# Attention products with the values stationary, two heads in the two 64-column halves of the array

## The reference, cut to what matters

```python
s = einsum('bghnqe,bghnke->bghnqk', qs, kb) * (Dh ** -0.5) + bias      # masked with -inf
p = exp(s - max(s)); l = sum(p)
o = einsum('bghnqk,bghnke->bghnqe', p / l, vb);  lse = m + log(l)
wts = softmax(stack(lses, axis=0), axis=0)        # over the 3 groups
y_a = sum(wts[..., None] * stack(outs, axis=0), axis=0)      # [256, 6 * 64]
merged = sigmoid(gate_a) * (y_a @ w_attn_proj) + sigmoid(gate_b) * (y_b @ w_ret_proj)
```

## Time and profile before

| | |
|---|---|
| median of 3 runs | 2450.14 us |
| lowest, highest | 2447.23, 2452.81 us |
| span of the profiled execution | 2447.4 us |
| busy in it | PE 2127.8, PEld 1525.4, DVE 785.8, ACT 703.8, POOL 1002.4 us |
| mean granted TensorE clock | 0.910 |
| attention of layer 0 (first scores to last ya) | 1372 to 1492 us |
| attention of layer 1 | 1947 to 2067 us |

### The profile page before, as it was taken

The page is one execution under the profiler, slowest core; times in us unless marked ns, Lnnn a source line. Parts: engine busy times, 40 slices in busy tenths (PEclk is TensorE's granted clock), DMA queues, the critical chain, the costliest instruction groups (busy, mean ns, idle before and its releaser), DMA issues.

```text
span 2447.4 us, 31903 instructions
## 1 busy us (share of the span) xinstructions
PE 2127.8 (87%) x13416; PEld 1525.4 (62%) x13416; DVE 785.8 (32%) x1516; ACT 703.8 (29%) x820; POOL 1002.4 (41%) x324
## 2 busy tenths in 40 slices
PE   7999988766777766776659999999999999999998
PEld 4788973333333333332318888887887887888887
DVE  4575752111111111111121435533312253634231
ACT  2246410000000000000004544544543453644442
POOL 1356530000000000000007765887887764786885
PEclk9999988788777888778879999999999999999999
DMA  9585479999999999999996544566656643555653
GB/s 329 152 282 164 156 325 399 428 428 428 428 428 428 428 428 428 428 428 428 428 390 226 174 130 121 180 189 194 209 191 199 215 157 115 172 175 182 206 188 136
DMA packets 248527, 680.56 MB, mean 278 GB/s; under 512 B 8622, under 2 KB 173504, under 8 KB 222883
## 3 DMA queue, kind: packets, MB, share of 16 engines
q1 hardware_dynamic: 244528, 672.41, 72.8%
q10 hardware_dynamic: 3075, 4.65, 0.7%
q0 software_dynamic: 816, 1.94, 0.3%
HBM read 674.38 MB, written 4.59 MB: 277 GB/s over the span
## 4 chain that ended last, share of the span: by engine, by line
PE 61%; DMA 29%; DVE 4%; POOL 2%; ACT 1%; issue 1%; SPq 1%; DVEq 0%; ACTq 0%
PE bank L2007 60%; DMA arena_sb<-w_exp 19%; DMA ring_sb<-w_exp 9%; POOL ring_parts L818 2%; PE bank L2010 2%; DMA ring_sb<-w_in 1%; DVE arena_sb L1209 1%; SPq L674 1%; ACT ring_parts L1073 1%; DVE bank L1212 1%; DVE bank L1209 1%; DVE x_sb L1212 0%; DVE sm_sb L1765 0%; DVE sm_sb L1879 0%; SPq L697 0%
## 5 line engine op out<-in xcount | busy, mean ns | idle before, releaser
L818 POOL TENSOR_TENSOR ring_parts<-ring_sb,ring_parts 128x2048 fp32r<-128x2048 f32 x186 | 847.3, 4573 | 1249.6 <-ACT ring_parts L1073 1249.3
L2007 PE MATMUL bank<-arena_sb 128*32 128x512 f32 (+9 forms) x3006 | 398.9, 552 | 122.7 <-DMA arena_sb<-w_exp 104.2
L2007 PE MATMUL bank<-arena_parts,ring_parts 128*128 128x256 f32 (+1 forms) x2480 | 450.1, 330 | 0.9 <-DVE arena_parts L1209 0.9
L2007 PE MATMUL bank<-hT_parts,ring_parts 128*128 128x256 f32 (+1 forms) x2208 | 431.0, 326 | 2.6 <-POOL ring_parts L818 2.6
L2007 PEld LDWEIGHTS bank<-arena_parts,ring_parts 128*128 128x128 f32 x2480 | 382.5, 189 | 50.2 <-DVE arena_parts L1209 1.1
L1073 ACT CAST ring_parts<-ring_sb 128x2048 fp32r<-128x2048 f32 x186 | 349.8, 1887 | 183.6 <-DMA ring_sb<-w_in 55.6
L2007 PE MATMUL bank<-ring_sb,arena_sb 128*32 128x512 f32 (+1 forms) x2240 | 266.8, 620 | 141.3 <-DMA ring_sb<-w_exp 138.2
L2007 PEld LDWEIGHTS bank<-hT_parts,ring_parts 128*128 128x128 f32 x2208 | 352.7, 190 | 41.9 <-POOL ring_parts L818 4.4
L1209 DVE TENSOR_TENSOR arena_sb<-bank,arena_sb 128x512 f32<-128x512 f32 (+5 forms) x244 | 141.3, 601 | 734.9 <-PE bank L2007 633.1
L2007 PEld LDWEIGHTS bank<-arena_sb 128*32 128x32 f32 (+4 forms) x3006 | 173.1, 153 | 315.0 <-DMA arena_sb<-w_exp 143.9
L2007 PE MATMUL bank<-ring_parts,arena_parts 128*128 128x512 f32 (+1 forms) x1248 | 285.0, 386 | 0.0
(11 more groups left out here) (252 smaller groups left out, 1285.2 us busy)
## 6 DMA issues: line engine op xcount, KB each, us to landing
ring_sb<-w_exp SPq DMA_DIRECT2D x96, 2048.0 KB, 35.5
arena_sb<-w_exp SPq DMA_DIRECT2D x94, 2048.0 KB, 35.6
ring_sb<-w_in SPq DMA_DIRECT2D x92, 1024.0 KB, 5.3
ring_sb<-w_ada SPq DMA_DIRECT2D x24, 1024.0 KB, 10.0
ring_sb<-w_ffn_gate SPq DMA_DIRECT2D x22, 1024.0 KB, 5.4
ring_sb<-w_ffn_up SPq DMA_DIRECT2D x22, 1024.0 KB, 5.3
ring_sb<-w_ffn_down SPq DMA_DIRECT2D x22, 1024.0 KB, 4.9
ring_sb<-w_in SPq DMA_DIRECT2D x42, 512.0 KB, 4.9
```

The lines of the kernel that those rows point to most:

```text
L818: g.tensor_tensor(low, half(n)[0], high.bitcast(F32), ALU.subtract).then_inc(s["lo_ready"], 1)
L2007: return M.matmul(o, l, r, start=first, stop=last)
```

## The change

The pair of heads 2p and 2p+1 becomes one unit `attn{l}.{p}`. `attention(p)` makes the values stationary (64 columns of `va` per head and key half) and moves the transposed probabilities (256 columns for the first key half, 128 for the second). Head 2p goes into partitions 0 to 63 of the bank, head 2p+1 into 64 to 127, that is into the two column halves of the array: 12 matmuls. Four more, with `ones` stationary and a diagonal of the inverse row sums moving, spread the inverses over the 64 partitions of each head. DVE makes the diagonals (two multiplications of `ident` by a column per head), then copies the inverses out of the bank, multiplies, and writes both parts of `yaTp` directly. `yaT` is gone. `pT` becomes six pieces of 384 columns (two heads), the places of the maxima and sums are doubled (`soft`), and DVE takes the maxima of both heads of a pair one after the other.

```diff
@@ layer_units
             units.add(f"score{l}.{j // 2}", 6, "V")
             if j:
-                units.add(f"attn{l}.{j - 1}", 1, "V")
+                units.add(f"attn{l}.{j // 2 - 1}", 1, "V")
...
-        if j % 2:
-            units.add(f"attn{l}.{j - 1}", 1, "V")
         units.add(f"pT{l}.{j}", 3, "A")
     units.add(f"rs{l}.0", 1, "V")
-    units.add(f"attn{l}.{HPG - 1}", 1, "V")
+    units.add(f"attn{l}.{HPG // 2 - 1}", 1, "V")
     units.add(f"rs{l}.1", 1, "V")
-    units.add(f"yaT{l}", 2, "V")
@@ tiles
+        pT = (tuple(arena[:, 22016 + 384 * i:22400 + 384 * i] for i in range(3)),
+              (hT_2[:, 1152:1536], hT_2[:, 1536:1920], b_rows[:, 0:384]))
+        inv_diag = sm[:, 128:640].rearrange("p (n t q) -> p n t q", n=2, t=2)
+        soft = (sm[:, 56:64], sm[:, 112:120])
@@ ACT, softmax_exp
-                        A.activation(sc[:, 0:3], sc[:, 0:3], ACT.Exp, bias=sm[:, 58:59], accum_out=sm[:, 60:61])
+                        v = soft[j % 2]
+                        A.activation(sc[:, 0:3], sc[:, 0:3], ACT.Exp, bias=v[:, 2:3], accum_out=v[:, 4:5])
...
@@ DVE
-                def attention_out(j):
+                def attention_out(p):
-                    b = take(f"attn{l}.{j}")
-                    for t in range(2):
-                        ins = V.tensor_scalar(ya[:, t, j * AD:(j + 1) * AD], b[:, t * AD:(t + 1) * AD], sm[:, 62 + t:63 + t], None, ALU.mult)
-                    give(ins)
+                    b = take(f"attn{l}.{p}")
+                    y = b[:, 0:T]
+                    inverse = inv_diag[:, 0].rearrange("p t q -> p (t q)")
+                    link(V.tensor_copy(inverse, b[:, T:2 * T]))
+                    link(tt(y, y, inverse))
+                    link(V.tensor_copy(yaTp[0][:, p], y))
+                    give(tt(yaTp[1][:, p], y, yaTp[0][:, p].bitcast(F32), ALU.subtract))
...
-                    sc = score[j % 2]
-                    V.tensor_reduce(sm[:, 56:57], sc[:, 0:3], AX.XY, ALU.max)
-                    link(V.tensor_reduce(sm[:, 57:58], sc[:, 3:9], AX.XY, ALU.max))
-                    link(V.tensor_scalar(sm[:, 58:60], sm[:, 56:58], -1.0, None, ALU.mult))
-                    dve.sem_inc(s["sc_ready"], 1)
-                    if j and j % 2 == 0:
-                        attention_out(j - 1)
+                        for sc, v in zip(score, soft):
+                            V.tensor_reduce(v[:, 0:1], sc[:, 0:3], AX.XY, ALU.max)
+                            link(V.tensor_reduce(v[:, 1:2], sc[:, 3:9], AX.XY, ALU.max))
+                            link(V.tensor_scalar(v[:, 2:4], v[:, 0:2], -1.0, None, ALU.mult))
+                            dve.sem_inc(s["sc_ready"], 1)
+                        if j:
+                            attention_out(j // 2 - 1)
...
-                    if j % 2:
-                        attention_out(j - 1)
                     dve.wait_ge(s["exp_done"], HPG * l + j + 1)
-                    if j:
-                        dve.wait_ge(s["freed_dve"], U.count[U.at(f"attn{l}.{j - 1}")])
-                    link(V.reciprocal(sm[:, 62:64], sm[:, 60:62]))
+                    v = soft[j % 2]
+                    link(V.reciprocal(v[:, 6:8], v[:, 4:6]))
+                    for t in range(2):
+                        ins = V.tensor_scalar(inv_diag[:, j % 2, t], ident[:], v[:, 6 + t:7 + t], None, ALU.mult)
+                    ins.then_inc(s["diag_ready"], 1)
...
@@ PE
-                def attention(j):
+                def attention(p):
-                    wait_emptied(pe, f"pT{l}.{j}")
-                    if j == 0:
+                    for n in range(2):
+                        wait_emptied(pe, f"pT{l}.{2 * p + n}")
+                    if p == 0:
                         wait_emptied(pe, f"va{l}")
-                    b = open_unit(f"attn{l}.{j}")
+                    b = open_unit(f"attn{l}.{p}")
+                    terms = [(g, kt_) for g in range(NG) for kt_ in ((0, 1) if g < NG - 1 else (1, 0))]
+                    for i, (g, kt_) in enumerate(terms):
+                        for n in range(2):
+                            c = (HPG * g + 2 * p + n) * AD
+                            mm(b[AD * n:AD * n + AD, kt_ * P:T], va[:, kt_, c:c + AD], pT[n][g][:, kt_ * T:T + kt_ * P],
+                               i == 0, i == len(terms) - 1)
+                    pe.wait_ge(s["diag_ready"], HPG * l + 2 * p + 2)
                     for t in range(2):
-                        terms = [(g, kt_) for g in range(NG) for kt_ in range(t + 1)]
-                        for n, (g, kt_) in enumerate(terms):
-                            c = (HPG * g + j) * AD
-                            blk = g if t == 0 else 3 + 2 * g + kt_
-                            ins = mm(b[:, t * AD:(t + 1) * AD], pT[:, blk], va[:, kt_, c:c + AD], n == 0, n == len(terms) - 1)
+                        for n in range(2):
+                            ins = mm(b[AD * n:AD * n + AD, T + t * P:T + (t + 1) * P], ones[:, 0:AD], inv_diag[:, n, t])
                     close(ins)
...
                     if j and j % 2 == 0:
-                        attention(j - 1)
+                        attention(j // 2 - 1)
...
-                    if j % 2:
-                        attention(j - 1)
                     pe.wait_ge(s["exp_done"], HPG * l + j + 1)
...
-                attention(HPG - 1)
+                attention(HPG // 2 - 1)
                 scores_r(1)
-                wait_emptied(pe, f"attn{l}.{HPG - 1}")
-                for i in range(2):
-                    b = open_unit(f"yaT{l}", i)
...
```

More of the change, by code:

```diff
@@ L38 @@
 ARENA = 29800
-PART_PLACES = ((0, 11264), (11264, 10256), (22016, 768), (23936, 768), (25640, 3160))
+PART_PLACES = ((0, 11264), (11264, 10256), (23168, 1536), (25640, 3160))
 HYC = 512
@@ L378, in kernel_program @@
         rm = region(20864, 2, 2, T)
-        pT = region(22016, 9, P)
-        ya = region(23168, 2, 384)
         decay = region(24704, RH, 384)
@@ L394, in kernel_program @@
                     for v in (hT_r[:].rearrange("p (k t) -> p k t", k=KD), parts(26752, KD)))
-        yaTp = (parts(23936, 3), parts(22016, 3))
+        yaTp = (parts(23936, 3), parts(23168, 3))
         ybTp = tuple(v.rearrange("p k t -> p (k t)").rearrange("p (k s t) -> p k s t", k=8, s=2)
@@ L470, in kernel_program @@
             lo_ready x_hi out_saved y_ready exp_done x_done yr_ready sc_ready
-            soft_arg sg_turned hT_turned aff_exp router_scaled vb_landed spared folded""".split()
+            soft_arg sg_turned hT_turned aff_exp router_scaled vb_landed spared folded diag_ready""".split()
         s = {n: sem(n) for n in names}
@@ L1145, in softmax_exp @@
                         act.wait_ge(s["sc_ready"], HPG * l + j + 1)
-                        A.activation(sc[:, 0:3], sc[:, 0:3], ACT.Exp, bias=sm[:, 58:59], accum_out=sm[:, 60:61])
-                        A.activation(sc[:, 3:9], sc[:, 3:9], ACT.Exp, bias=sm[:, 59:60],
-                                     accum_out=sm[:, 61:62]).then_inc(s["exp_done"], 1)
+                        v = soft[j % 2]
+                        A.activation(sc[:, 0:3], sc[:, 0:3], ACT.Exp, bias=v[:, 2:3], accum_out=v[:, 4:5])
+                        A.activation(sc[:, 3:9], sc[:, 3:9], ACT.Exp, bias=v[:, 3:4],
+                                     accum_out=v[:, 5:6]).then_inc(s["exp_done"], 1)
                     softmax_exp()
@@ L1153, in _ @@
                         b = take2(f"pT{l}.{j}", i)
-                        give(A.copy(pT[:, 3 * i:3 * i + 3].rearrange("p k t -> p (k t)"), b[:, 0:384]))
+                        give(A.copy(pT[j % 2][i], b[:, 0:384]))
                 for h in range(RH):
@@ L1913, in _ @@
                 decayed(0)
-                attention_out(HPG - 1)
+                attention_out(HPG // 2 - 1)
                 decayed(1)
-                for i, (c0, c1) in enumerate(((0, 2), (2, 3))):
-                    b = take(f"yaT{l}", i)[:, 0:(c1 - c0) * T]
-                    link(V.tensor_copy(yaTp[0][:, c0:c1].rearrange("p k t -> p (k t)"), b))
-                    give(tt(yaTp[1][:, c0:c1].rearrange("p k t -> p (k t)"), b,
-                            yaTp[0][:, c0:c1].rearrange("p k t -> p (k t)").bitcast(F32), ALU.subtract))
                 for h in range(2, RH):
@@ L2611, in _ @@
                         for q in range(3):
-                            ins = tr(b[:, q * P:(q + 1) * P], score[j % 2][:, 3 * i + q])
+                            ins = tr(b[:, q * P:(q + 1) * P], score[j % 2][:, (i, 3 + 2 * i, 4 + 2 * i)[q]])
                         close(ins)
@@ L2623, in _ @@
                 scores_r(0)
-                attention(HPG - 1)
+                attention(HPG // 2 - 1)
                 scores_r(1)
-                wait_emptied(pe, f"attn{l}.{HPG - 1}")
-                for i in range(2):
-                    b = open_unit(f"yaT{l}", i)
-                    for q in range(2 - i):
-                        for t in range(2):
```

(4 more changed lines are left out.)

## The result

| | before | after |
|---|---|---|
| median of the runs | 2449.06 us (2447.23 to 2452.81, 4 runs) | 2437.74 us (2435.63 to 2439.81, 4 runs) |
| ratio, 95% interval | | 0.9948 [0.9937, 0.996] |
| span of the profiled execution | 2447.4 us | 2437.3 us |
| one layer's attention on PE, first score matmul to first gate half (layer 0 / 1) | 132.47 / 132.46 us | 126.54 / 126.57 us |

The forecast was 2438.8 us. The last line of the table is the measure I use from here on. It repeats within 0.1 us between profiles of one kernel, whereas the start of the stage moves: 1372.19 us in the profile of before, 1373.93 after, 1376.77 in a second profile of the same changed kernel. That scatter is made ahead of the attention, and two profiles of one kernel show it as well.

The account below looks back on a forecast made before the run. PE was taken to bound the kernel (61% of the chain, DMA 29%). Per layer -0.3 + 1.4 + 2.15 + 2.4 = 5.65 us, two layers 11.3 us, giving 2438.8 us; own range 2435 to 2442, overall 2432 to 2448.

Parts of the forecast that it names:

- pair block: PE's 12 products and four spreading products for two heads, taken at the scores' column rate: 2.65 us.
- E to the end of the pair block, heads 2 and 3: From PE ending the last half before this place (E) to the pair's last product: 7.7 us, 0.3 later than before.
- wait at the fourth score unit: Scores of heads 2 and 3: PE newly waits 1.7 us for DVE to empty the bank this unit needs.
- scores of heads 2, 3: First place in a layer: 0.3 us lost, although 2.07 us of PE work went.
- scores of heads 4, 5: Second place in a layer: old products 2.07 + 2.00 us replaced by 2.65, 1.4 us gained.
- POOL waits: PE's waits for POOL's low parts: two of three go through earlier maxima, 1.0 + 1.4 = 2.4 us a layer.
- behind head 5: Third place in a layer: two old attention products and the `yaT` transposes replaced by 2.65 us, 2.15 us gained.
- The diagonals cost nothing: DVE's two multiplications per head, 0.3 us each, are covered by other work and ready for PE: 0 us.
- Loads bare in column tiles: Rival, 5%: weight loads in the pair's products are not hidden, 4.49 us a pair, 2449.8 us, no change.
- halves that exclude each other: Rival, 4%: the array's column halves do not overlap and loads are bare too, 6.57 us a pair, 2462.3 us.
- Cheaper than thought: Rival, 12%: pair blocks take 2.36 us and no wait at the fourth score unit, 2433.7 us.
- The locked diagonals: Rival, 10%: POOL locks out DVE's diagonals at the score places, some 2 us on PE at four places, 2446.8 us.

Follow-up runs that it names:

- the filler: Changed kernel with `attention(0)` put between the first two and last four score units of heads 2 and 3: 2435.48 us, 125.16 us a layer.

## Why the prediction was right

The forecast missed by 1.1 us. That is better than the evidence allows, and in part luck: single runs of the changed kernel spread over 4 us, and the forecast was counted from 2450.14 us, where the kernel before took 2449.06 beside the changed one. The gains compare as 11.3 us forecast, 11.3 between the medians and 11.8 in the two layers. The layers test the steps.

Here is what the steps measured in layer 0, from the starts of the groups on PEld:

| step | forecast | measured |
|---|---|---|
| pair block | 2.65 us | 2.54, 2.54, 2.53 us |
| E to the end of the pair block, heads 2 and 3 | 7.7 us | 7.76 us |
| wait at the fourth score unit | 1.7 us | 1.67 (PEld), 1.51 (PE) |
| scores of heads 2, 3 | -0.3 | -0.33 |
| scores of heads 4, 5 | +1.4 | 88.78 - 81.35 = 7.43 to 84.78 - 78.78 = 6.00: +1.43 |
| POOL waits | +2.4 | 1.27 + 1.64 = +2.91 |
| behind head 5 | +2.15 | 43.66 to 41.73: +1.93 |
| a layer | 5.65 | 5.94 (5.93 on PE) |

For heads 4 and 5 the numbers are distances from the layer's first score load; behind head 5 they run from the end of that place to the first gate half. Two errors of opposite sign stand in the table: the POOL waits were worth 0.5 us more, and behind head 5 there was 0.2 us less, though the pair block was 0.1 us shorter. There the transposes and the first `scores_r` take 2.61 us (1481.39 to 1484.00), against about 2.3 before, an estimate, since the 34 loads are one row. Why is open.

- *The halves run at once.* Shown by the same products in one half (+1.92 us a pair). The scores' rate was the right row to take. Its 2816 columns at one rate hide a difference, though: products 1.99 us for 2304 columns, spread 0.54 for 512.
- *The removed `attention(0)` had covered DVE.* Shown by the wait, which DVE's operation ends, and by the filler, which takes its place. This is why three pairs of products save 3.0 us a layer and not 4.5.
- *Two POOL waits go with the early maxima.* Shown by the early maxima alone. The term was 0.5 us too small: it took PE's idle time for the price of the wait, and rows overlap.
- *The diagonals cost nothing.* True in this arrangement, and shown by three times as many. For heads 0 to 3 the reason was right too: at head 1 the prediction had POOL's run over 2.1 us ahead of the pair (1410.8 and 1412.9), and the profile has 1412.83 and 1414.78, 2.0 us apart. For heads 4 and 5 it was wrong. It announced 0.3 us for each diagonal and looked only at what must be ready for PE, but both pairs meet POOL and take 1.93 and 1.71 us. What hides the last one is 1.5 us of slack on PE's side behind head 5, and with the maxima late it is used up.
- *The rivals.* Loads bare in column tiles, and halves that exclude each other, fell with the pair block; the first would have made it 4.49 us. It is what the rule of the Trainium skill in the prediction ("TensorE: Matmul & The Clock Gate", Part 3) would give, and the trace disagrees with 2.54 us. Cheaper than thought fell with the wait. The POOL waits stayed only where the maxima stayed late. The locked diagonals are real, but cost 1.7 us (1.46 in PE's row) at one place a layer and not 2 us at four, and only in that arrangement.

The sum holds for the change as a whole: 2.91 us from the early maxima (2.92 alone) and 3.03 from the three places. It would have been wrong for the half of the change with late maxima. Before running it I expected 2442.5 us and measured 2450.2. Of the 3.03 us, 0.73 go to longer POOL waits, since the even head's diagonals then stand ahead of the odd head's maxima, and 1.68 to the held diagonals of head 5, which leaves 0.6. The prediction had priced neither.

## What to carry to other kernels

Before counting a removed block as a gain, ask which engine was working under it: here 2.07 us of products covered a DVE chain, and 0.33 us were lost where they went. Here the inputs of the faster engine had to come earlier as well, or most of the gain turned into waits; a small reorder that makes inputs ready sooner can be what lets the large change pay. Where a wait is left, look for independent work that can stand in it, and put concurrent tiles next to each other in the program: head after head, 1.35 us of each block's overlap was lost.

## What the runs showed of the hardware

- Two 64-column halves with all 128 rows, in float32 and with a load for each matmul, ran 2304 columns in 1.99 us, against 3.87 by the serial rate, but only when the two heads alternated; in turn the block took 1.35 us more. Both heads in one half took 4.04 us for 2.10.
- A diagonal (`tensor_scalar`, or `tensor_tensor` with both inputs in SBUF) that started while POOL worked was held until POOL's operation ended, and two in a row could be held twice (4.96 us for 0.48 us of work). Maxima and inverses from SBUF, and `tensor_tensor` with an input in the bank, passed a busy POOL at their usual length.
- Waits of 1.01 and 1.38 us in PE's rows cost 1.28 and 1.64 us of the stage: matmul rows overlap by 0.16 us where there is no wait, and the group behind a wait takes 0.1 us longer.
